# Feed-forward halves of a transformer block reordered: two products, two blocks of the next chunk, four products, two blocks, one product

## The reference, cut to what matters

```python
h2 = modulate(rmsnorm(x, norm_mlp_g[l]), shift2, scale2)      # 512 x 2048
y = jnp.square(jax.nn.relu(h2 @ w_ff1[l])) @ w_ff2[l]         # w_ff1: 2048 x 8192, w_ff2: 8192 x 2048
x = x + gate2 * y
```

## Time and profile before

| | |
|---|---|
| median of 3 runs | 2301.58 us (2297.93 to 2303.14) |
| the profiled execution's own time | 2301.29 us |
| its span | 2299.5 us |
| PE busy | 2235.5 us, 97% |
| DVE busy | 1506.9 us, 66% |
| POOL busy | 1242.9 us, 54% |
| ACT busy | 828.4 us, 36% |

### The profile page before, as it was taken

One profiled execution on the slowest core, in us unless ns is written; L12 is line 12 of the kernel. 1 busy time (PEld: TensorE's weight loads), 2 busy tenths in 40 slices (PEclk: granted clock), 3 DMA queues, 4 the chain that ended last, 5 costly groups with the idle time before them and its releaser, 6 DMA issues.

```text
span 2299.5 us, 26259 instructions
## 1 busy us (share of the span) xinstructions
PE 2235.5 (97%) x10217; PEld 1861.4 (81%) x10217; DVE 1506.9 (66%) x1506; ACT 828.4 (36%) x1108; POOL 1242.9 (54%) x528
## 2 busy tenths in 40 slices
PE   5999999999998999999999999999999999999998
PEld 4778888888887788788888888888888888888887
DVE  5969877665655377355686676677666556646746
ACT  3235444433345322243333333333333333333331
POOL 1014444442431254357777776777767677667763
PEclk8999999999998999999999999999999999999999
DMA  9875345556657485434434333343433333333342
GB/s 339 314 270 173 125 167 174 181 183 219 224 185 273 139 293 208 150 126 127 147 107 138 131 129 120 128 134 123 137 110 93 105 104 102 110 97 112 94 174 92
DMA packets 185752, 365.50 MB, mean 159 GB/s; under 512 B 15386, under 2 KB 40476, under 8 KB 183840
## 3 DMA queue, kind: packets, MB, share of 16 engines
q1 hardware_dynamic: 176848, 340.79, 44.5%
q10 hardware_dynamic: 8784, 23.07, 2.6%
HBM read 332.33 MB, written 31.48 MB: 158 GB/s over the span
## 4 chain that ended last, share of the span: by engine, by line
PE 86%; DVE 9%; issue 2%; DMA 2%; SPq 1%; ACT 1%; POOL 0%; ACTq 0%; DVEq 0%; POOLq 0%
PE ps L813 19%; PE ps L814 19%; PE ps L815 19%; PE ps L1267 8%; PE ps L1268 8%; PE ps L1269 8%; DVE acc L1866 2%; DMA araw<-in_w_ada 1%; PE ps L847 1%; PE ps L884 1%; DVE accx L1989 1%; PE ps L1070 1%; DVE rt L2130 1%; DVE yc L2037 0%; DMA o_d<-yc 0%
## 5 line engine op out<-in xcount | busy, mean ns | idle before, releaser
L371 POOL TENSOR_TENSOR wlo<-wraw,whi 128x1024 fp32r<-128x1024 f32 (+3 forms) x120 | 300.9, 2521 | 447.6 <-ACT whi L366 427.5
L805 POOL TENSOR_TENSOR wlo<-wq,whi 128x1024 fp32r<-128x1024 f32 x150 | 386.5, 2579 | 119.9 <-ACT whi L1758 119.9
L813 PE MATMUL ps<-h2T,whi 128*128 128x512 f32 x1024 | 399.7, 390 | 2.5 <-DVE h2T L2397 2.5
L805 POOL TENSOR_TENSOR wlo<-wraw,whi 128x1024 fp32r<-128x1024 f32 x132 | 381.0, 2887 | 38.2 <-ACT whi L1758 38.2
L814 PE MATMUL ps<-h2T,whi 128*128 128x512 f32 x1024 | 399.2, 390 | 0.0
L815 PE MATMUL ps<-h2T,wlo 128*128 128x512 f32 x1024 | 399.1, 390 | 0.0
L2468 DVE TENSOR_TENSOR yacc<-ps,yacc 128x1024 f32<-128x1024 f32 x202 | 246.5, 1220 | 222.0 <-PE ps L1269 219.5
L1267 PE MATMUL ps<-whi,ahi 128*128 128x512 f32 x840 | 326.9, 389 | 1.1 <-DVE yacc L2468 1.1
L1269 PE MATMUL ps<-whi,alo 128*128 128x512 f32 x840 | 326.8, 389 | 0.0
L1268 PE MATMUL ps<-wlo,ahi 128*128 128x512 f32 x840 | 326.8, 389 | 0.0
L1758 ACT ACTIVATE whi<-wq 128x1024 fp32r<-128x1024 f32 x150 | 159.1, 1061 | 352.8 <-PE ps L815 222.9
(11 more groups left out here) (321 smaller groups left out, 3967.9 us busy)
## 6 DMA issues: line engine op xcount, KB each, us to landing
wraw<-in_w_ff SPq DMA_DIRECT2D x136, 512.0 KB, 3.8
araw<-in_w_ada SPq DMA_DIRECT2D x128, 512.0 KB, 5.3
wq<-in_w_ff SPq DMA_DIRECT2D x120, 512.0 KB, 4.2
wraw<-in_w_in SPq DMA_DIRECT2D x72, 512.0 KB, 5.9
arawx<-in_w_ada SPq DMA_DIRECT2D x64, 512.0 KB, 4.6
wraw<-in_w_out SPq DMA_DIRECT2D x32, 512.0 KB, 6.1
xnat<-in_x ACTq DMA_DIRECT2D x4, 1024.0 KB, 7.6
xT_d<-xT ACTq DMA_DIRECT2D x1, 4096.0 KB, 13.5
```

The lines of the kernel that those rows point to most:

```text
L371: pool.tensor_tensor(wlo[:, slot, 0:kb, 0:cols], wraw[:, slot, 0:kb, 0:cols], whi[:, slot, 0:kb, 0:cols].bitcast(F), ALU.subtract).then_in ...
L805: pool.tensor_tensor(wlo[:, slot, :, :], raw, whi[:, slot, :, :].bitcast(F), ALU.subtract).then_inc(lo_ready, 1)
L813: pe.matmul(dst, lhs[0], rhs[0], start=start, stop=False)
```

## The change

`half_order(h)` gives another order for halves 0 to 28. With f0 to f3 for the four F blocks: before W0 W1 f0 W2 W3 f1 W4 W5 f2 W6 f3, now W0 W1 f0 f1 W2 W3 W4 W5 f2 f3 W6. So f1 goes ahead of W2 and W3, and f3 ahead of W6. Since halves follow each other, W6 of a half is now directly followed by W0 and W1 of the next. PE, ACT and POOL go by this order, SP's loads and their waits use the places in it; DVE's instructions stay in their order.

```diff
     f = ff1_of(h)
     if len(f) == 2:
         return w[:4] + f[:1] + w[4:6] + f[1:] + w[6:]
-    return w[:2] + f[:1] + w[2:4] + f[1:2] + w[4:6] + f[2:3] + w[6:] + f[3:]
+    return w[:2] + f[:2] + w[2:6] + f[2:] + w[6:]
```

## The result

| | before | changed |
|---|---|---|
| median | 2299.76 us (2297.78 to 2303.14, 4 runs) | 2317.27 us (2314.80 to 2320.94, 4 runs) |
| ratio | 1 | 1.0076, 95% interval 1.0058 to 1.0095 |
| profiled execution, its span | 2301.29, 2299.5 us | 2315.37, 2313.6 us |

The change makes the kernel slower by 0.76%. The forecast was 2315.7 us, 0.6% slower: inside the wider range of 2308 to 2321 us, but the median lies 0.3 us above the forecast's own range of 2313 to 2317.

What follows compares the result with a forecast made beforehand. PE was taken as saturated, with at most about 1.1 us to gain. The profiled 2301.3 us plus 11.1 (odd halves) and 3.3 (half 29) gave 2315.7 us, 0.6% slower; own range 2313 to 2317, wider range 2308 to 2321.

Steps and rivals of the forecast that it cites:

- Bound: PE in the feed-forward halves: busy 100.00 of 100 us, so the change can gain at most about 1.1 us.
- Weights at nothing: Weight blocks from ACT and POOL: slots lead by at least 8.16 us, so four products in a row cost nothing.
- The 14 odd halves: Odd halves 1 to 27: product 5 waits for DVE's late sum 3, 0.79 us each, 11.1 us in all.
- Product 6 beside the next half: Border of halves: odd halves' squares end at 5.2 us, f0 begins at 5.44; costed at nothing, upper bound 5 us.
- rival 3: Further DVE waits, above all late squares stopping f0 some 0.3 us, 14 times: 2320 us; chance 10%.
- Half 29: Last half: `relu` begins 4.53 us after the border instead of 1.23, so PE resumes 3.3 us later.
- rival 4: PE's clock falls in half 29 after standing still 3.6 us, losing 2.5 us: 2318 us; chance 6%.
- clock 1.00: Sign expected in the new profile: PE's granted clock stays at 1.00.
- No stall: Odd halves: product 5 is never late, no measurable change, only half 29 costs: 2304.6 us; chance 8%.
- flipped turns: Odd halves: POOL's split goes before DVE's operand sum, product 5 3.3 us late, 48 us, 2353 in all; chance 4%.
- a gain: PE: fewer changes between kinds of block would pay; only half 29's 1.1 us is there; chance 2%.
- rival 1: Odd halves: POOL's split begins over 0.6 us later, DVE's low part takes 0.68 us, product 5 never late; chance 8%.

Runs made afterwards that it cites:

- The version that takes most of it back: Kernel before the change, with DVE's sum of product 1 moved ahead of the last of half 29's four low parts: 2298.16 us, ratio 0.9992.
- sum 3 first: Changed kernel, with DVE's sum of product 3 moved ahead of the low part of the next chunk's second operand in odd halves: 2304.39 us, ratio 1.0018.
- POOL yields: Changed kernel, with POOL's split of f2 in odd halves waiting until DVE's low part is done: 2303.54 us, ratio 1.0012.
- second swap alone: Kernel before the change, with only f3 moved ahead of product 6, and f1 left in its old place: 2312.89 us, ratio 1.0058.
- half 28 old: Changed kernel, with half 28 put back in the old order of blocks: 2313.03 us, ratio 1.0056.

## Why the prediction was right

- **Bound.** PE saturated, 1.1 us at most to gain: as said. The version that takes most of it back gains 1.2, the wait and its refill.
- **Weights at nothing.** Right: in the changed kernel PE never waits for POOL.
- **The 14 odd halves, 11.1 us.** The place, the count, the wait for sum 3 and the 2.9 us of the low part came out as read from before. Each costs 0.80 us, forecast 0.79; in all 11.2. That the offsets carry over unchanged was the step that could have failed; both tests of the cause (sum 3 first, POOL yields) confirm it.
- **Product 6 beside the next half, at nothing.** Right in the full change: no F block waits, and in half 1 the four squares end at 1074.56 + 2.64 = 1077.20, 0.33 us before f0 begins at 1077.53. But the need was misread. f0 waits for one square for each bank (`ff1_block`), so at 5.44 us only the first of the four has to be done. With the second swap alone, where `relu` comes later, f0 of half 1 begins at 1076.44 without a wait and the squares end at 1075.16 + 2.65 = 1077.81. Only the gate sums of halves 9 and 17 need all four, and they wait 1.27 us there. The stop of 0.3 us in rival 3 rests on the same misreading.
- **Half 29, 3.3 us.** 3.27 measured; `relu` 4.50 us after the border, forecast 4.53.
- **The clock.** This is rival 4, which I gave 6% and 2.5 us, and it came true beside the forecast: the clock fell, for a net 1.6 us. All four traces with a stop of 3.4 us in half 29 show a fall, for 0.3 us in three of them, so the 6% were much too low, and 1.6 is the price in one trace and not a fixed cost. It was wrong to take the stop of 2.5 us at 2265 us for reassurance: at that very place five of the eleven traces show a fall. And ahead of the first F block the granted clock was 0.50 from 960.2 to 970.4 us, twice the 5 us that the window of the earlier trace rows showed, from within the first stop of 2.1 us on. The sign "clock 1.00" failed.
- **The sum.** With the measured terms it is 2301.3 + 11.2 + 3.3 + 1.6 = 2317.4 us, against a median of 2317.27. The forecast of 2315.7 lacked the clock. Part of the agreement is luck: the medians differ by 17.5 us, the profiled executions by 14.1 and the way by 15.7, and a forecast built on the median of before (2299.76) would have been 1.5 us lower. The nearness to the profiled execution (2315.37) owes something to the 1.7 us that this one was shorter elsewhere.
- **Other rivals.** No stall, flipped turns, further waits and a gain did not happen in the changed kernel. That DVE gets its turn if POOL's split comes later (rival 1's point of decision) was made to happen by the wait on POOL.

## What to carry to other kernels

With a saturated TensorE the order of blocks is worth what the engines behind it can serve, so one lists for each block when its inputs are needed and when each helper answers, and moves nothing that leaves less than the longest wait of a helper. On DVE, operations that take turns with POOL go behind the ones that TensorE waits for and that do not take turns, as long as TensorE does not need their own results next (the four low parts of half 29 cost 4.9 us of waiting); where several stand together, they go where POOL is idle. At the ends of a loop, where the order changes kind, the same move can cost more than in the middle: here one half of 30 took 4.9 of 15.7 us.

## What was not expected of the hardware

- A stop of 3.43 us was followed by the lower clock in four of four traces, with different prices. In the full change the fall began 0.7 us before PE resumed and lasted 6.8 us, and the first matmul took 0.77 us. With the second swap alone, sum 3 first and POOL yields (3.44, 3.44 and 3.43 us) it began 1.2, 0.2 and 0.3 us after PE had resumed and lasted 3.4 us. The net price was 1.6 us in the first case and 0.3 in the others.
- A stop of 2.5 us at PE's last wait came with a fall of 3.4 us in five of eleven traces (it began 0.5 us before PE resumed in one and 0.8 to 1.4 us after in four), and these five take 1.4 to 1.6 us more from there to the end.
- A stop of only 1.27 us, followed by 16 one-column matmuls, came before a fall of 3.4 us in both places where it happened, 3.3 and 3.0 us after PE had resumed. The same matmuls without the stop had none.
- After a stop TensorE needs about 0.1 us more for the next 12 matmuls at full clock (2.85 us before, 2.81 with half 28 old, against 2.72).
